# Latent attention's heads: keys on partitions, three rounded passes, sums of exponentials on GpSimd

## The reference, cut to what matters

```python
def queries(cq, rotate):
    q = (_rms(cq) * q_norm) @ w_uq
    q = _rms(q.reshape(*q.shape[:2], MLA_HEADS, MLA_QK)) * q_gain
    return _rope_tail(q, cos, sin) if rotate else q
...
def one_block(qi):
    s = jnp.einsum('bqhd,bkhd->bhqk', qi, k).astype(jnp.float32) * scale
    p = jax.nn.softmax(s, axis=-1).astype(v.dtype)
    return jnp.einsum('bhqk,bkhd->bqhd', p, v)
```

## Time and profile before

| what | us |
|---|---|
| median of 3 runs | 3508.5 |
| the profiled execution, its own time | 3506.41 |
| its span | 3505.1 |
| TensorE busy / weight loads busy | 3292.2 / 2630.5 |
| VectorE busy | 1721.1 |
| ScalarE busy | 1313.9 |
| GpSimd busy | 1056.1 |

### The profile page before, as it was taken

One profiled execution on the slowest core, in us unless ns is written; L12 is line 12 of the kernel. 1 busy time (PEld: TensorE's weight loads), 2 busy tenths in 40 slices (PEclk: granted clock), 3 DMA queues, 4 the chain that ended last, 5 costly groups with the idle time before them and its releaser, 6 DMA issues.

```text
span 3505.1 us, 44707 instructions
## 1 busy us (share of the span) xinstructions
PE 3292.2 (94%) x17128; PEld 2630.5 (75%) x17128; DVE 1721.1 (49%) x3172; ACT 1313.9 (37%) x2278; POOL 1056.1 (30%) x513
## 2 busy tenths in 40 slices
PE   8999999999999998999898899999999988889999
PEld 6677777777867776777786677888988556668877
DVE  5348345423138635532798655222565655543234
ACT  4333334333333333333423433222443455533332
POOL 3123122234303222124336432232553000034443
PEclk9999899999999999999999999999999999999999
DMA  5532121132562122124222001122332100022222
GB/s 183 182 136 81 40 81 65 53 101 99 180 221 77 47 70 84 41 70 141 67 67 67 1 31 61 61 67 67 112 117 82 40 35 1 4 71 91 99 96 79
DMA packets 87479, 286.41 MB, mean 82 GB/s; under 512 B 9697, under 2 KB 20321, under 8 KB 86497
## 3 DMA queue, kind: packets, MB, share of 16 engines
q1 hardware_dynamic: 85968, 272.67, 22.9%
q10 hardware_dynamic: 1296, 10.88, 0.8%
HBM read 279.32 MB, written 4.19 MB: 81 GB/s over the span
## 4 chain that ended last, share of the span: by engine, by line
PE 54%; DVE 7%; ACT 3%; issue 2%; POOL 0%; DMA 0%; DVEq 0%; ACTq 0%; POOLq 0%
PE psum L318 14%; PE psum L319 14%; PE psum L320 14%; PE psum L317 9%; PE psum L3768 1%; DVE mla_cols L3857 1%; PE psum L3756 1%; PE psum L1192 1%; DVE padded L2806 0%; DVE h_low L582 0%; DVE ml_weights L3209 0%; PE psum L3734 0%; DVE squares L511 0%; ACT weights_high L395 0%; ACT mla_probs L3813 0%
## 5 line engine op out<-in xcount | busy, mean ns | idle before, releaser
L413 POOL TENSOR_TENSOR weights_low<-weights_loaded,weights_high 128x1024 fp32r<-128x1024 f32 (+3 forms) x456 | 958.6, 2102 | 2362.7 <-ACT weights_high L395 2277.6
L318 PE MATMUL psum<-h_high,weights_high 128*128 128x512 f32 (+1 forms) x2384 | 900.4, 378 | 45.5 <-DVE h_low L582 21.2
L319 PE MATMUL psum<-h_low,weights_high 128*128 128x512 f32 (+1 forms) x2384 | 882.6, 370 | 0.0
L320 PE MATMUL psum<-h_high,weights_low 128*128 128x512 f32 (+1 forms) x2384 | 881.7, 370 | 0.0
L395 ACT CAST weights_high<-weights_loaded 128x1024 fp32r<-128x1024 f32 (+3 forms) x456 | 422.0, 926 | 472.7 <-PE psum L320 398.3
L318 PEld LDWEIGHTS psum<-h_high,weights_high 128*128 128x128 f32 x2384 | 456.1, 191 | 134.4 <-issue 35.7
L319 PEld LDWEIGHTS psum<-h_low,weights_high 128*128 128x128 f32 x2384 | 455.7, 191 | 77.4 <-issue 4.1
L320 PEld LDWEIGHTS psum<-h_high,weights_low 128*128 128x128 f32 x2384 | 454.6, 191 | 76.6
L318 PE MATMUL psum<-act_high,weights_high 128*128 128x512 f32 (+1 forms) x528 | 187.7, 355 | 8.2 <-DVE act_low L4155 6.2
L319 PE MATMUL psum<-act_low,weights_high 128*128 128x512 f32 (+1 forms) x528 | 187.5, 355 | 0.0
L320 PE MATMUL psum<-act_high,weights_low 128*128 128x512 f32 (+1 forms) x528 | 187.4, 355 | 0.0
(11 more groups left out here) (506 smaller groups left out, 5307.9 us busy)
## 6 DMA issues: line engine op xcount, KB each, us to landing
weights_loaded<-stream_dram SPq DMA_DIRECT2D x468, 512.0 KB, 3.3
weights_loaded<-stream_dram SPq DMA_DIRECT2D x80, 128.0 KB, 2.3
weights_loaded<-stream_dram SPq DMA_DIRECT2D x24, 384.0 KB, 3.0
weights_loaded<-stream_dram SPq DMA_DIRECT2D x8, 272.0 KB, 4.9
x<-x_dram SPq DMA_DIRECT2D x4, 512.0 KB, 6.6
arena_mem<-mem_dram ACTq DMA_DIRECT2D x2, 1024.0 KB, 4.9
x<-x_dram ACTq DMA_DIRECT2D x1, 2048.0 KB, 9.1
x_kept_dram<-x ACTq DMA_DIRECT2D x1, 2048.0 KB, 9.6
```

What stands on the lines that cost most here:

```text
L318: pe.matmul(out, a.high, b.high, start=start, stop=False)
L319: pe.matmul(out, a.high, b.low, start=False, stop=False)
L320: return pe.matmul(out, a.low, b.high, start=False, stop=stop)
L413: pool.tensor_tensor(self.low[s][:, 0:size], raw[:, 0:size], self.high[s][:, 0:size], ALU.subtract).then_inc(*g.event("weights_low").up(po ...
```

## The change

The score tile is turned: 128 keys on partitions by 512 queries (`scores`), so the exponentials are already in the form that `weigh` needs, and the transposes and their copies go. For it the features are split into high and low; a 97th row holds ones for the keys and the negative maximum for the queries, so the exponential has neither bias nor scale. The queries are multiplied by their scale beforehand (`scaled_queries`, first pair on VectorE, others on GpSimd). The maximum ("limit") comes from a product of the high parts alone, in 8 matmuls of 128 queries by 384 keys per head, reduced by VectorE (`limit`), combined, transposed to a row by 4 matmuls and written by ScalarE (`row`). `edges` fills the constant 97th rows on ScalarE. `head_steps` spreads the next pair's preparation over the 12 tiles of a pair; `first_steps` does it for the first pair ahead of all tiles. Weighing is done four tiles at a time, 512 queries wide, with one bank for a pair's output. GpSimd adds the exponentials of a head over the key tiles (`add`), `totals` sums over partitions with a matrix of ones, and VectorE takes the reciprocal of the 128x512 totals and multiplies (`finish`). There are five probability buffers. The removed lines are those printed above; of the new ones the wait instructions behind each `for m in g.after(...)`, blank lines and small index helpers are left out. `weighted_high_scalar` now waits for `("mla_out", j)`.

```diff
--- before.py
+++ after.py
@@ -3700,7 +3700,8 @@
...
+    dve.tensor_scalar(t.rq[:, :], t.rq[:, :], MLA_QK ** -0.5, None, ALU.mult).then_inc(*S("root").up(dve, "mla_rq"))
+    scaled_queries(g, dve, 0)
@@ -3708,197 +3709,270 @@
...
+TILES = [(i, 2 * k + b) for k in range(TT // 2) for i in range(2) for b in range(2)]
+PER_PAIR, BURST = len(TILES), 4
+N_PROBS, HALF_KEYS = 5, TOK // 2
+FEATURE_BANKS, LIMIT_BANKS, OUT_BANK = (5, 7), (3, 4), 6
+def head_steps(n):
+    features = {0: [(0, 0), (0, 1)], 1: [(0, 2)], 2: [(1, 0)], 3: [(1, 1)], 4: [(1, 2)]}
+    limits = {4: [0, 1], 5: [2, 3], 6: [4, 5], 7: [6, 7], 8: [8, 9], 9: [10, 11], 10: [12, 13], 11: [14, 15]}
+    return ([("features", i, step) for i, step in features.get(n, [])]
+            + [("limit", x // 8, x % 8) for x in limits.get(n, [])]
+            + ([("row", 0, 0)] if n == 10 else []))
+def first_steps():
+    return ([("features", i, step) for i in range(2) for step in range(3)] + [("limit", 0, x) for x in range(8)]
+            + [("row", 0, 0)] + [("limit", 1, x) for x in range(8)])
...
+    return n + 1 if TILES[n % PER_PAIR][1] == 0 else n
...
 def heads_tensor(g):
...
+    g.features_turn, g.limits_turn = 0, 0
+    def features_bank(key):
+        g.features_turn += 1
+        return g.claim(key, FEATURE_BANKS[g.features_turn % 2])
+    def step_tensor(pair, what, i, x):
+        h = 2 * pair + i
+        if what == "features":
+            key, c = ("features", h, x), h // MLA_PER
+            b = features_bank(key)
+            for m in g.after(pe, S("k_done").at(c) if which == "k" else S("q_scaled").at(pair)):
...
+        elif what == "limit":
+            key, q, lo = ("limit", h, x), x // 2, x % 2 * HALF_KEYS
+            g.limits_turn += 1
+            b = g.claim(key, LIMIT_BANKS[g.limits_turn % 2])
+            for m in g.after(pe, *(S("feature_high").at((h, step)) for step in range(3))):
...
+            pe.matmul(g.banks(b)[:, 0:HALF_KEYS], t.q_feat[h % 4].high[0:MLA_QK, q * P:(q + 1) * P],
+                      t.k_feat[h % 4].high[0:MLA_QK, lo:lo + HALF_KEYS], start=True, stop=True).then_inc(
+                *S("projected").up(pe, key))
+        else:
+            key = ("limit_row", h)
+            b = features_bank(key)
+            for m in g.after(pe, S("limited").at(h)):
...
+            for q in range(QT):
+                done = pe.transpose(g.banks(b)[0:1, q * P:(q + 1) * P], t.limits[h % 2][:, 0, q:q + 1], g.ident)
+            done.then_inc(*S("projected").up(pe, key))
+    def scores(pair, n):
+        i, kt = TILES[n]
+        h, key = 2 * pair + i, ("mla_tile", pair * PER_PAIR + n)
+        b = g.claim(key, key[1] % 3)
+        own = [S("drained").at(("features", h, step)) for step in range(3)]
+        own += [S("drained").at(("limit_row", h)), S("edged").at(0)]
+        for m in g.after(pe, *own):
...
+        mm(g, g.banks(b), t.k_feat[h % 4][:, kt * P:(kt + 1) * P], t.q_feat[h % 4][:, :], True, True).then_inc(
+            *S("scored").up(pe, key))
+    def weigh(pair, k):
+        key = ("mla_out", pair)
+        if k == 0:
+            g.claim(key, OUT_BANK)
+        for kt in (2 * k, 2 * k + 1):
+            for i in range(2):
+                n = tile_of(pair, i, kt)
+                for m in g.after(pe, S("drained").at(("mla_tile", n))):
...
+                done = pe.matmul(g.banks(OUT_BANK)[MLA_V * i:MLA_V * (i + 1), :], t.vt[:, kt, 2 * pair + i, :],
+                                 probs_slot(t, n)[:, :], start=kt == 0, stop=kt == TT - 1, tile_position=(0, MLA_V * i))
+        done.then_inc(*S("weighed").up(pe, ("mla", pair, k)))
+    def totals(pair):
+        key = ("mla_total", pair)
+        b = features_bank(key)
+        for i in range(2):
+            for m in g.after(pe, S("added").at(tile_of(pair, i, TT - 1))):
...
+            done = pe.matmul(g.banks(b)[MLA_V * i:MLA_V * (i + 1), :], g.ones[:, 0:MLA_V], t.mla_sums[i][:, :],
+                             start=True, stop=True, tile_position=(0, MLA_V * i))
...
+    for what, i, x in first_steps():
+        step_tensor(0, what, i, x)
+    for pair in range(PAIRS + 1):
+        for n in range(PER_PAIR if pair < PAIRS else BURST):
+            if pair < PAIRS:
+                scores(pair, n)
+            if n % BURST == 0 and pair + n:
+                at = (pair * PER_PAIR + n) // BURST - 1
+                weigh(at // (TT // 2), at % (TT // 2))
+            if pair < PAIRS and n == 0:
+                step_tensor(pair, "row", 1, 0)
+            if pair and n == BURST - 1:
+                totals(pair - 1)
+            if pair + 1 < PAIRS:
+                for what, i, x in head_steps(n):
+                    step_tensor(pair + 1, what, i, x)
 def heads_scalar(g):
...
+    def edges():
+        one = g.ones[0:1, 0:1]
+        for h in range(4):
+            for part, n, scale in ((t.k_feat[h].high, TOK, 1.0), (t.k_feat[h].low, TOK, 0.0), (t.q_feat[h].low, SEQ, 0.0)):
+                ones = bass.AP(tensor=one.tensor, offset=one.offset, ap=[[one.ap[0][0], 1], [0, n]])
+                for m in g.after(act, S("head_sums").at(GROUPS * (TT + QT) - 1)):
...
+                act.activation(part[MLA_QK:MLA_QK + 1, :], ones, ACT.Copy, scale=scale).then_inc(*S("edged").up(act, 0))
+    def step_scalar(pair, what, i, x):
+        h = 2 * pair + i
+        if what == "features":
+            key, at = ("features", h, x), slice(tiles[0] * P, (tiles[-1] + 1) * P)
+            dst, gain = (t.k_feat, g.small.k_gain_col) if which == "k" else (t.q_feat, g.small.q_gain_col)
+            freed = [S("scored").at(("mla_tile", (pair - 1) * PER_PAIR - 1))] if pair >= 2 else []
+            for m in g.after(act, S("projected").at(key), *freed):
...
+            act.activation(dst[h % 4].high[0:MLA_QK, at], g.bank(key)[0:MLA_QK, 0:len(tiles) * P], ACT.Copy,
+                           scale=gain).then_inc(*S("feature_high").up(act, (h, x)))
+        elif what == "row":
+            key = ("limit_row", h)
+            for m in g.after(act, S("projected").at(key)):
...
+            act.activation(t.q_feat[h % 4].high[MLA_QK:MLA_QK + 1, :], g.bank(key)[0:1, 0:SEQ], ACT.Copy,
+                           scale=-1.0).then_inc(*S("drained").up(act, key))
+    def exponentials(n):
+        key, freed = ("mla_tile", n), []
+        if n >= N_PROBS:
+            pair, at = (n - N_PROBS) // PER_PAIR, (n - N_PROBS) % PER_PAIR // BURST
+            freed = [S("weighed").at(("mla", pair, at)), S("added").at(added_with(n - N_PROBS))]
+        for m in g.after(act, S("scored").at(key), *freed):
...
+        act.activation(probs_slot(t, n)[:, :], g.bank(key), ACT.Exp).then_inc(*S("drained").up(act, key))
+    g.weights.note("mla_heads")
+    edges()
+    for what, i, x in first_steps():
+        step_scalar(0, what, i, x)
+    for pair in range(PAIRS):
+        for n in range(PER_PAIR):
+            exponentials(pair * PER_PAIR + n)
+            if n == 0:
+                step_scalar(pair, "row", 1, 0)
+            if pair + 1 < PAIRS:
+                for what, i, x in head_steps(n):
+                    step_scalar(pair + 1, what, i, x)
+            elif 3 <= n < 3 + PAIRS - 1:
+                weighted_high_scalar(g, n - 3)
+                if n == 7:
+                    g.weights.round(("mla_w_out", 0))
 def heads_vector(g):
...
+    def step_vector(pair, what, i, x):
+        h = 2 * pair + i
+        if what == "features":
+            key, at = ("features", h, x), slice(tiles[0] * P, (tiles[-1] + 1) * P)
+            dst, gain = (t.k_feat, g.small.k_gain_col) if which == "k" else (t.q_feat, g.small.q_gain_col)
+            part = dst[h % 4][0:MLA_QK, at]
+            for m in g.after(dve, S("feature_high").at((h, x))):
...
+            dve.scalar_tensor_tensor(part.low, g.bank(key)[0:MLA_QK, 0:len(tiles) * P], gain, part.high, ALU.mult,
+                                     ALU.subtract).then_inc(*S("drained").up(dve, key))
+        elif what == "limit":
+            key, c = ("limit", h, x), t.limits[h % 2]
+            freed = [S("projected").at(("limit_row", h - 2))] if h >= 2 else []
+            for m in g.after(dve, S("projected").at(key), *freed):
...
+            dve.tensor_reduce(c[:, x % 2, x // 2:x // 2 + 1], g.bank(key)[:, 0:HALF_KEYS], AX_X, ALU.max).then_inc(
+                *S("drained").up(dve, key))
+            if x == 7:
+                for m in g.after(dve):
...
+                dve.tensor_tensor(c[:, 0, :], c[:, 0, :], c[:, 1, :], ALU.max).then_inc(*S("limited").up(dve, h))
+    def finish(pair):
+        key, out = ("mla_total", pair), t.mla_out[:, pair, :]
+        for m in g.after(dve, S("projected").at(key)):
...
+        dve.reciprocal(out, g.bank(key)).then_inc(*S("drained").up(dve, key))
+        for m in g.after(dve, S("weighed").at(("mla", pair, TT // 2 - 1))):
...
+        dve.tensor_tensor(out, g.banks(OUT_BANK), out, ALU.mult).then_inc(*S("drained").up(dve, ("mla_out", pair)))
+    for what, i, x in first_steps():
+        step_vector(0, what, i, x)
```

(93 more changed lines are left out.)

148 lines of the change are left out of this document (20 added, 128 removed).

## The result

| what | before | after |
|---|---|---|
| median, us (range; runs) | 3507.94 (3503.15 to 3514.27; 4) | 3532.29 (3528.81 to 3534.85; 4) |
| ratio to before, 95% interval | | 1.0075 [1.006, 1.0091] |
| profiled execution / its span | 3506.41 / 3505.1 | 3532.65 / 3531.3 |

A forecast was written before the change was run, and what follows sets the result against it. TensorE, with work in 94% of the span, was taken as the bound. +24 +2 -5 -4 -8 = +9 on 3506.4 gave 3515, or 3517 us as a median; range 3486 to 3532, slower at 0.48.

The forecast's parts named there:

- Entry: Ahead of the first score tile: one-row copies, features and limits put that tile at 2860.4, 24 us later: +24 us.
- First pair: The first pair of heads has no burst, totals or reciprocal of a pair before it: -5 us.
- the +2: After the nearly idle entry, TensorE's clock is probably low when the first tiles start: +2 us.
- half clock: Low TensorE clock after its wait in each pair: 1.1 us on average; the burst alone costs 1.7 us more.
- The steady pair: Each repeated pair of heads takes 28.8 us against 29.35, bounds 25 and 29.5; seven pairs save 4 us.
- The wait itself: TensorE stands 3.4 us a pair while VectorE's 3.5 us reciprocal and the product hold the bank the next burst claims.
- rival D: Low clock lasts through limits and tiles after the wait, a further 1.7 us a pair, +12: 3529 us; chance 0.18.
- the pair at full clock: A steady pair, followed from its first tile, ends at 27.7 us before the low clock is added.
- Sixth reciprocal to the projection: Covers the last pair and exit, forecast at 31 us against 39.0: -8 us, bounds -13 and -3.
- B: The reciprocal costs as a plain operation, pair 24.9 us with no clock loss: 3487 us; chance 0.20.
- C: Wait is 3.4 us but the clock holds and limits overlap tiles better, pair 27 us: 3504 us; chance 0.22.
- upper bounds of the entry: Ahead of the first score tile, slower low parts would make the entry 27 us later instead of 24.

The follow-up runs named there:

- e4: Kernel after with 13 more matmuls, results unused, issued ahead of the burst where TensorE waits, in six pairs: 3527.06 us, ratio 1.0064 to before.
- e2: Kernel after with ScalarE copying the finished sums out of the output bank at once, so the reciprocal no longer holds it: 3514.91 us, ratio 1.0033 to before.
- e3: Kernel after with the reciprocal replaced by a plain copy, the division left out: 3506.31 us, ratio 1.0004 to before.
- e5: On top of e2, totals made as columns, reciprocal over 128x8, spread to 512 columns by identity matmuls: 3514.05 us, ratio 1.002 to before.

## Why the prediction was right in sign and 15 us off in size

The profiled difference is +26.2, of which 24.8 are there at the first projection matmul, against +9 forecast. Its steps, in order:

1. **Entry: right.** First tile 2862.15 where 2860.4 was worked out. Copies 839 and 627 ns (I had 0.84 and 0.62: a one-row copy costs its columns), features done by 2850.6, then each head's eight reductions in 5.4 us. 1.7 us more.
2. **First pair: 2.9 us shorter than worked out.** 32.4 us from the first tile to the first reciprocal, where 28.8 - 5 + 2 and the 9.5 to the reciprocal's place make 35.3; the clock in it was 0.96, half of full for its first 2.5 us alone, so of the +2 at most 1.3 was due; and the 28.8 has in it the 1.1 for half clock behind a wait that the first pair does not have.
3. **The steady pair: the step that failed.** The wait itself is as forecast (reciprocal 3358 ns for 3.5, TensorE waits 3.0 for 3.4). The price of what follows was not. In the five steps from the first reciprocal to the sixth, 159.0 us, forecast 5 x 28.8 = 144:
   - half clock: 159.0 less 5 x 28.65 is 15.8, or 3.2 a pair, where I took 1.1 as a mean between nothing and a burst at half speed: **+10.3 us**. It was not only the burst: limits, a feature step and often the next burst ran slow as well, which is what rival D describes (1.7 more a pair; its sum of 3529 is the nearest of the four to the 3532 measured). Filling the wait took part of it away (0.95, in one execution of e4), but e2 has 0.88 and e3 0.93 without a wait of 3 us, so what else brings it stays open. The mean itself could be read from the trace of before: TensorE has seven waits of 3 to 5 us in it, and with each comes a half-clock stretch of 3.4 to 10.2 us, 6.3 on average, worth some 3.2 us of work (an estimate, half of it).
   - the pair at full clock: 28.65 for 27.7, **+4.8 us**. Candidates, not tested one by one: bursts took 1.87 for 1.72 (four rounds in 1.85 us, the line of the earlier trace rows, would have given 1.85), totals 1.07 for 0.9, and the two maxima of 128x4 took 588 ns each on average, not 160, while GpSimd adds.
4. **Sixth reciprocal to the projection: +2.0.** 26.6 + 25.75 from the sixth reciprocal to the projection, against 28.8 - 9.5 + 31 = 50.3. The timeline of the exit shows two things that I had named but given no price of their own: ScalarE's three weight casts, 3.2 us, delay an exponential for which TensorE waits 1.86 us, and the low parts meet the additions (4.64 us for three). The first is on the chain of waits, the second is not:

```profile
3091.02 4.64 DVE L3984 TENSOR_TENSOR mla_out_low<-mla_latents,mla_out_high 128x512 fp32r<-128x512 f32 x3 [5.31 <-ACT mla_out_high L3977]
...
3093.51 3.20 ACT L395 CAST weights_high<-weights_loaded 128x1024 fp32r<-128x1024 f32 x3
...
3097.39 0.50 PE L318 MATMUL psum<-q_feat_high,k_feat_high 97*128 97x512 f32 x1 [1.86 <-ACT context L3871]
```

1.7 - 2.9 + 15.0 + 2.0 is 15.8, the whole of 24.8 less 9.

**The rivals.** B (a cheap reciprocal, 3487) fell by the 3358 ns; e3 also shows that even so the kernel would have stood at 3506: B's pair of 24.9 takes 26.0 at full clock in e3, and B left the half clock out, where e3 has 0.93. C (the clock holds, pair of 27) fell by 0.90, though e5 reaches such a pair, 27.2, without the long reciprocal. Its argument was thin: of the 14 waits of 1.8 to 2.3 us in the trace of before, six left no mark in the clock, but eight did. The range was too narrow on the slow side: D and the upper bounds of the entry could come together.

**The reciprocal and the additions.** A slope of about 6.5 ns an element, read from three small sizes in the earlier trace rows, gave 3.5 us, and the trace has 3.36, 4.9 times the 692 ns of e3's copy of the same tile. The Trainium skill, VectorE: DVE Perf Modes, section "First, the fixed hardware budget", has the reciprocal as an iterated divide with a repeat count of 8; the estimate of 4.3 us worked out from that was 0.9 too high, and the trace agrees with it in kind only. In the groups above, the 128x4 maximum with both inputs in SBUF takes 588 ns on average and 160 ns at 2855.99, when GpSimd was idle, and the product with an input in PSUM keeps its 692. This agrees with the Trainium skill, SBUF — State Buffer, section "Who interferes with whom": a VectorE instruction with two inputs in SBUF contends with a GpSimd instruction that reads SBUF, one with at most one such input doesn't.

## What to carry to other kernels

Price a wait of the engine that bounds the kernel with what its clock does behind it, and bound that from above by everything that follows up to the next steady stretch, not by the next instruction alone: here, with 3.0 us of waiting a pair, the half clock cost another 3.2 on average, between nothing and 6. Before dividing a wide tile on VectorE, divide the few numbers that it repeats and spread them with a matmul (3358 ns to 207, for 1.7 us of TensorE; with it a pair went from 29 to 27.2 us, and the kernel gained less than that for what it lost elsewhere). And when preparation moves ahead of a loop, look which of its steps the first item really needs last: moving the constant rows by six steps gave back 8 of 24 us.

## What the runs showed of the hardware that I had not expected

- VectorE's reciprocal of 128x512 float32 takes 3358 ns with its input in PSUM (after), and of 128x8 207 ns (e5): 6.25 ns for each element more.
- The mean clock changes the stage's time with no change in the work: 0.98 against 0.91 over the same 802 matmuls was 163.7 against 170.8 us, and it came alike, 0.91, in the profiles of two kernels that share the changed bank order.
- The same wait of TensorE, 2.98 or 2.99 us in six pairs of after, is followed by 0 to 13.7 us at half clock before the next totals; and the clock can be lower without such a wait (0.88 in e2) than with it (0.90).
- A plain float32 matmul instruction of one column with 128 columns of weights costs 0.12 us in a row of 16 (1.91 us, e5), as much as one of 128 columns did in the estimate from the earlier trace rows: a narrow output saves nothing here.
